# DeltaNet projections of one hybrid layer as seven half-size block products per slab, with sums and joining on VectorE

## The reference, cut to what matters

```python
proj = x @ w_in                        # x 256x2048, w_in 2048 x 18496
qkv = silu(causal_depthwise_conv(qkv, conv_w))           # 4 taps
q = l2_normalize(qkv[..., :2048] per head of 128)
k = l2_normalize(qkv[..., 2048:4096] per head of 128)
v = qkv[..., 4096:]                    # 32 heads of 128
...
o = chunked_gated_delta_rule(q, k, v, g, beta)
o = o * rsqrt(mean(square(o), axis=-1) + 1e-6)
o = o * norm_w * silu(z)               # z: another 4096 columns of proj
return o.reshape(...) @ w_dn_out
...
y = gelu(s5 output); (y @ w_glu_a) * sigmoid(y @ w_glu_b)    # the GLU stage
```

## Time and profile before

| | |
|---|---|
| median of 3 executions | 2885.38 us (2883.77 to 2957.61) |
| the profiled execution's own time | 2883.57 us |
| its span in the trace | 2881.8 us |
| mean granted TensorE clock | 0.995 of full speed (2.4 GHz) |
| TensorE busy | 2823.4 us, 98% of the span |
| weight loads busy | 2060.2 us, 71% |
| VectorE busy | 1038.6 us, 36% |
| ScalarE busy | 488.3 us, 17% |
| GpSimd busy | 75.2 us, 3% |

### The profile page before, as it was taken

The page is one execution under the profiler, slowest core; times in us unless marked ns, Lnnn a source line. Parts: engine busy times, 40 slices in busy tenths (PEclk is TensorE's granted clock), DMA queues, the critical chain, the costliest instruction groups (busy, mean ns, idle before and its releaser), DMA issues.

```text
span 2881.8 us, 50108 instructions
## 1 busy us (share of the span) xinstructions
PE 2823.4 (98%) x20775; PEld 2060.2 (71%) x20775; DVE 1038.6 (36%) x2273; ACT 488.3 (17%) x805; POOL 75.2 (3%) x119
## 2 busy tenths in 40 slices
PE   8999999999999999999989999999999999999997
PEld 7888888888888888888889999863444444434442
DVE  2433424424334306777765653221111121112114
ACT  2221232212312121110010000121111211112110
POOL 1000000000000000000010000000000000000000
PEclk9999999999999999999999999999999999999999
DMA  7243342332424534344447657277999999999997
GB/s 206 83 132 93 104 127 89 118 118 89 147 89 105 161 93 142 118 139 128 145 156 230 204 172 265 102 310 325 392 422 422 422 422 422 422 422 422 422 422 281
DMA packets 328853, 654.13 MB, mean 227 GB/s; under 512 B 45232, under 2 KB 274736, under 8 KB 279536
## 3 DMA queue, kind: packets, MB, share of 16 engines
q1 hardware_dynamic: 328688, 651.61, 61.6%
HBM read 649.49 MB, written 2.10 MB: 226 GB/s over the span
## 4 chain that ended last, share of the span: by engine, by line
PE 71%; issue 16%; DMA 7%; DVE 2%; DVEq 1%; POOLq 1%; SPq 1%; ACT 1%; ACTq 0%; POOL 0%
PE bank L670 14%; PE bank L999 10%; PE bank L1191 9%; PE bank L920 8%; PE bank L1229 7%; DMA arena<-in_w_up_dram 7%; PE bank L1170 4%; PE bank L1056 4%; PE bank L1269 4%; PE bank L746 1%; PE bank L764 1%; PE bank L757 1%; PE bank L883 1%; PE bank L1201 1%; POOLq L605 1%
## 5 line engine op out<-in xcount | busy, mean ns | idle before, releaser
L670 PE MATMUL bank<-arena 128*128 128x256 f32 x4096 | 931.1, 382 | 0.0
L670 PEld LDWEIGHTS bank<-arena 128*128 128x128 f32 x4096 | 763.7, 190 | 111.1 <-issue 7.6
L1191 PE MATMUL bank<-arena 128*64 128x512 f32 x2048 | 445.6, 594 | 12.5 <-DMA arena<-in_w_up_dram 12.5
L1191 PEld LDWEIGHTS bank<-arena 128*64 128x64 f32 x2048 | 144.3, 137 | 311.7 <-issue 281.6
L999 PE MATMUL bank<-arena 128*128 128x128 f32 x2576 | 290.1, 276 | 6.0 <-DVEq L1969 6.0
L999 PEld LDWEIGHTS bank<-arena 128*128 128x128 f32 x2576 | 289.9, 193 | 6.3 <-DVEq L1969 6.2
L920 PE MATMUL bank<-arena 128*128 128x256 f32 x1024 | 223.5, 380 | 0.0
L920 PEld LDWEIGHTS bank<-arena 128*128 128x128 f32 x1024 | 194.1, 190 | 26.6
L1229 PE MATMUL bank<-arena 128*64 128x512 f32 x960 | 209.3, 594 | 0.5 <-ACT arena L1580 0.5
L2229 DVE TENSOR_SCALAR arena<-bank 128x512 f32<-128x512 f32 x16 | 11.1, 691 | 463.2 <-PE bank L1191 463.2
L1229 PEld LDWEIGHTS bank<-arena 128*64 128x64 f32 x960 | 67.5, 137 | 131.7 <-issue 131.0
(11 more groups left out here) (336 smaller groups left out, 2076.7 us busy)
## 6 DMA issues: line engine op xcount, KB each, us to landing
arena<-in_w_in_dram SPq DMA_DIRECT2D x72, 2048.0 KB, 8.7
arena<-in_w_up_dram SPq DMA_DIRECT2D x64, 2048.0 KB, 16.5
arena<-in_w_gate_dram SPq DMA_DIRECT2D x64, 2048.0 KB, 13.9
arena<-in_w_down_dram SPq DMA_DIRECT2D x64, 2048.0 KB, 21.1
arena<-in_w_dn_out_dram SPq DMA_DIRECT2D x16, 2048.0 KB, 8.1
arena<-in_w_glu_b_dram SPq DMA_DIRECT2D x8, 2048.0 KB, 8.1
arena<-in_w_glu_a_dram SPq DMA_DIRECT2D x8, 2048.0 KB, 8.2
arena<-in_w_mix_out_dram SPq DMA_DIRECT2D x8, 2048.0 KB, 13.7
```

Source lines behind the costliest of these rows:

```text
L670: last = mm(ps[bank][:, ct * T:ct * T + T], ring[:, buf, k, ct * P:ct * P + P], rhs[:, k, :], start=k == 0, stop=k == KD - 1)
L1191: last = mm(ps[bank][CAP * o:CAP * o + CAP, :], xg[:, 4 * q + k, CAP * o:CAP * o + CAP], w[:, o, k], start=False, stop=q == 3 and k == 3, ...
```

## The change

Slabs 0 to 3 of each group are computed by seven block products each (`seven_heads`, 56 matmuls of 128 columns), with the parts in regions of banks 0, 1, 5, 6 and 1, 2, 0, 7. Their weight sums are built on VectorE (`sums`; for slab 0 of the next group in three pieces within the apply part, for slab 1 before the last scaling, for slabs 2 and 3 between the convolutions), the token sums of x once at the start (`token_sums`), and `join_heads` adds the parts up into `dn_joined` in SBUF, from which `conv` now reads. z slabs stay as they were.

The outputs of the apply part are now made with tokens on the partitions (operands swapped). So the sum of squares is a reduction on VectorE over ScalarE's squares (no product with ones), its rsqrt works on 8 elements per partition, VectorE scales into `otok`, and TensorE turns the eight blocks (`turn_outputs`) behind slab 0 of the next group. In the GLU stage the token sums of x move from GpSimd to VectorE, behind the weight sums of the second slab. The first load of the S5 slabs is issued ahead of the small S5 loads. VectorE's loop over the groups is written as seven turns and a last one.

```diff
+            def turn_outputs(g):
+                pe.wait_ge(apply_dve, 4 * g + 4)
+                for a in range(GV):
+                    for c in range(2):
+                        col = (a % 2) * T + c * P
+                        last = tr(ps[3 + a // 2][:, col:col + P], otok[:, c, a], ident[:, :])
+                last.then_inc(apply_pe, 1)
+
+            def seven_heads(g, r, lo, hi):
+                buf = r % RING
+                extra_w = dn_wsum[r % 2]
+                if lo == 0:
+                    pe.wait_ge(slot_loaded[buf], 16 * (2 * g + r // 3 + 1))
+                    pe.wait_ge(bank_taken[r % 3], 2 * g + r // 3 + 1)
...
+                table = ((0, weight(0, 0), plain(0, 0)), (1, weight(0, 1), plain(1, 0)),
+                         (6, summed(extra_w, 0), summed(dn_xsum, 0)), (2, summed(extra_w, 1), summed(dn_xsum, 1)),
+                         (5, weight(1, 0), summed(dn_xsum, 2)), (3, weight(1, 1), summed(dn_xsum, 3)),
+                         (4, summed(extra_w, 2), plain(1, 1)))
+                for i in range(lo, hi):
+                    if i == KD:
+                        pe.wait_ge(prepared, 4 * g + 2 + r)
+                    p, k = divmod(i, KD // 2)
...
             def front(g):
-                part(16 * (2 * g + 1), 0, 0, 2 * g, xT, 4, 2 * KD)
-                for r in range(1, 3):
-                    project(16 * (2 * g + 1), r, r, 2 * g, xT)
+                seven_heads(g, 0, 8, 56)
+                turn_outputs(g - 1)
+                seven_heads(g, 1, 0, 56)
+                seven_heads(g, 2, 0, 56)
...
-                part(16 * (2 * g + 2), 0, 0, 2 * g + 1, xT, 0, 18)
+                seven_heads(g, 3, 0, 36)
...
-                part(16 * (2 * g + 2), 0, 0, 2 * g + 1, xT, 18, 2 * KD)
+                seven_heads(g, 3, 36, 56)
                 pe.wait_ge(tok_taken, g + 1)
                 decay_products(1)
+                pe.wait_ge(bank_taken[2], 2 * g + 2)
                 z0(0, 19)
...
-                pe.wait_ge(osq_ready, g + 1)
-                for i in range(2):
-                    last = mm(ps[3 + i][:, :], ones[:, :], sq[:, i * 512:i * 512 + 512], start=True, stop=True)
-                last.then_inc(oss_ready, 1)
...
+            dve.wait_ge(xt_taken, 8)
+            token_sums(xT, dn_xsum)
+            sums(0, 0)
             dve.wait_ge(bd_ready, 1)
             dve.wait_ge(bias_loaded, 32)
...
             dve.sem_inc(glog_ready, 1)
+            sums(0, 1)
             dve.wait_ge(gcum_ready, 1)
...
+                join_heads(0)
                 conv(0)
+                sums(g, 2)
+                join_heads(1)
                 conv(1)
+                sums(g, 3)
+                join_heads(2)
                 conv(2)
...
                 decay(0)
+                join_heads(3)
                 conv(3)
                 decay(1)
...
+                if more:
+                    sums_one(g + 1, 0)
...
+                if more:
+                    sums_two(g + 1, 0)
...
+                if more:
+                    sums_three(g + 1, 0)
+
+                dve.wait_ge(osq_ready, g + 1)
+                V.tensor_reduce(osum, sq.rearrange("p (a t) -> p a t", t=P), AX_X, ALU.add)
+                dve.drain()
+                dve.sem_inc(oss_ready, 1)
                 dve.wait_ge(orn_ready, g + 1)
-                og = oT[:, ds(GV * g, GV), :]
-                V.tensor_tensor(og, og, rn.rearrange("p (a t) -> p a t", a=GV), ALU.mult)
-                dve.drain()
+                for c in range(2):
+                    V.tensor_tensor(otok[:, c], ps[7 - c][:, :].rearrange("p (a d) -> p a d", a=GV),
+                                    by_head(osum[:, GV * c:GV * c + GV], P), ALU.mult)
+                dve.drain()
+                dve.sem_inc(apply_dve, 1)
+                if more:
+                    sums(g + 1, 1)
                 dve.wait_ge(bank_taken[2], 2 * g + 3)
+                dve.wait_ge(apply_pe, 7 * g + 7)
...
-            weight_sums(1, 0, 1, True)
-            gelu_sums()
-            weight_sums(2, 0, 2, True)
+            weight_sums(0, 1, True)
+            dve.wait_ge(gelu_done, 1)
+            token_sums(uT, usum)
+            weight_sums(0, 2, True)
+            token_sums(xT, xsum)
             join(0, 1, True)
```

More of the change, by code:

```diff
@@ L161, in build @@
         zvT = at(w0 + 8192, GV, T)
+        dn_joined = at(w0, 512)
+        dn_partial = at(w0 + 512, 4, P)
+        dn_xsum = at(12288, 4, KD // 2, P)
+        dn_wsum = [at(w0 + 9216 + 3072 * i, 3, KD // 2, P) for i in range(2)]
+        regions = banks[:, :].rearrange("p (b n) -> p b n", n=P)
+        dn_first, dn_second = (0, 5, 1, 0), (1, 6, 2, 7)
         uT = at(SH, KD, T)
@@ L376, in _ @@
             sp.dma_start(dsk, d_skip.rearrange("(k a) q -> (a q) k", k=KD), allow_slow_non_contiguous=True).then_inc(s5_loaded, 16)
-            for r in range(3):
+            for r in range(1, 3):
                 load_slot((S_U + r) % RING, in_rows(w_in[:, SC * r:SC * r + SC]), r, U_USE)
@@ new lines, in seven_heads, with weight, plain, summed @@
+            def seven_heads(g, r, lo, hi):
[4 more added lines that the diff above has]
+                    pe.wait_ge(bank_taken[r % 3], 2 * g + r // 3 + 1)
+                    if r == 0:
+                        pe.wait_ge(bank_taken[1], 2 * g + 1)
+                    if r == 2:
+                        pe.wait_ge(bank_taken[0], 2 * g + 2)
+                        pe.wait_ge(bank_taken[1], 2 * g + 1)
+                    if r == 3:
+                        pe.wait_ge(kd_in, 1)
+                def weight(i, j):
+                    return lambda k: ring[:, buf, 8 * j + k, P * i:P * i + P]
+                def plain(i, j):
+                    return lambda k: xT[:, 8 * i + k, P * j:P * j + P]
+                def summed(v, i):
+                    return lambda k: v[:, i, k]
+                table = ((0, weight(0, 0), plain(0, 0)), (1, weight(0, 1), plain(1, 0)),
[6 more added lines that the diff above has]
+                    p, k = divmod(i, KD // 2)
+                    place, left, right = table[p]
+                    bank = dn_first[r] if place < 4 else dn_second[r]
+                    last = mm(regions[:, 4 * bank + place % 4], left(k), right(k), start=k == 0, stop=k == KD // 2 - 1)
+                if hi == 56:
+                    last.then_inc(bank_ready[r % 3], 1)
@@ L681, in group @@
+            def front(g):
+                seven_heads(g, 0, 8, 56)
+                turn_outputs(g - 1)
+                seven_heads(g, 1, 0, 56)
+                seven_heads(g, 2, 0, 56)
+            def group(g, more):
                 pe.wait_ge(sq_ready, g + 1)
@@ L1394, in _ @@
                 act.wait_ge(oss_ready, g + 1)
-                for i in range(2):
-                    A(rn[:, i * 512:i * 512 + 512], ps[3 + i][:, :], ACT.Ln, scale=1.0 / P, bias=eps_l2)
+                A(osum, osum, ACT.Ln, scale=1.0 / P, bias=eps_l2)
                 act.drain()
-                A(rn, rn, ACT.Exp, scale=-0.5).then_inc(orn_ready, 1)
+                A(osum, osum, ACT.Exp, scale=-0.5)
+                act.drain()
+                act.sem_inc(orn_ready, 1)
             act.sem_inc(phase_done[0], 1)
```

164 lines of the change are left out of this document (99 added, 65 removed).

## The result

The changed kernel takes 2870.05 us, the median of five executions (2868.29 to 2872.03), against 2885.38 us before: a ratio of 0.9949, 95% interval 0.9935 to 0.9962 (one slow execution of before, 2957.61 us, is left out of the ratio). It is faster by 15 us, where 36 were forecast, and 4 us outside the range.

The account below looks back on a forecast made before the run. TensorE's stream, busy 98% of the span, was taken as the bound. Savings of 41.6 + 6.0 + 6.0 less losses of 14.4 and 2.8 give 36.4 us, so 2849 us against 2885.38; 8-in-10 range 2833 to 2866 us.

Parts of the forecast that it names:

- The slab at 12.51 us: Slabs 0 to 3 of each group: 12.51 us each in seven products instead of 13.81, saving 41.6 us over 32 slabs.
- The outputs by token: Apply part's outputs: products with ones go (1.72 us per group), eight transposes come (0.97 us); 6.0 us saved.
- Weight sums at 1.23 us: Sign to look for: VectorE's weight sums run undisturbed at 1.23 us; sums over 2 us would show the prediction wrong.
- VectorE up by 214 us: Sign to look for: VectorE's busy time rises by some 27 us a group, about 220 us.
- `front`'s margins of 0.6 to 3.2 us: VectorE's sums, joins and scalings in `front` finish before TensorE wants them, with 0.6, 1.8 and 3.2 us to spare, costing nothing.
- the prologue: Start of the kernel: waits for decay biases (1.3 us) and for sums of slabs 1 and 2 (0.9, 0.6); 2.8 us lost.
- The joins in `front`: Sign to look for: VectorE's joins in `front` stand 12.5 us apart.
- The wait at the first level: Solve's first level: join(3) lengthens VectorE's chain, so TensorE's wait grows by 1.8 us per group; 14.4 us lost.
- rival (b): VectorE also late in `front` or at the scaling of q and k, 2 us per group more: 2865 us; chance 0.12.
- (c): New VectorE sums run at the disturbed 3.33 us beside GpSimd, not 1.23: 115 us more, 2964 us; chance 0.03.
- the term for the GLU stage: GLU stage: TensorE's 6.02 us wait for the token sums of y goes whole; 6.0 us saved.
- TensorE's rows follow each other without gaps: Within a group TensorE's stream is unbroken, the one wait being 0.20 us at the solve's first level.

Follow-up runs that it names:

- the delayed old kernel: Kernel before the change, with decay(1) computed three times over, which delays VectorE's chain to the solve's first level: 2907.48 us (1.008 of before).
- the filler in place: Changed kernel with TensorE's loop written out and four wide matmuls of z1 moved ahead of the transposes of v: 2829.71 us (0.9812 of before).

## Why the prediction was wrong

**What held.** The slab at 12.51 us and the 41.6 us from it. The outputs by token: 0.87 us of turns for 1.72 of products gives 6.8 us where I had 6.0. Weight sums at 1.23 us, VectorE up by 214 us, and `front`'s margins of 0.6 to 3.2 us: the sums' semaphore holds TensorE up only twice, 1.0 us in all, at 42 and 55 us, which are two terms of the prologue. (The joins in `front` stand 11.4 us apart and not 12.5 as I had written: behind a late first one VectorE works them off at its own pace.) The prologue: L734 comes at 64.43 us, 1.02 us earlier than L683 did, where 3.9 saved less 2.8 lost makes 1.1. The wait at the first level: 2.0 us in each group, 13.5 us more in all, where the sum had 14.4. Of rival (b), VectorE late in other places, no more was seen than that 1.0 us, though its 2865 us are nearest to the result; of (c), disturbed sums, nothing either.

**The sum left out what a wait costs behind it.** The step reads "the wait grows by 1.8 us per group: 14.4 us lost". The wait was right, but seven times TensorE then ran at the 1.2 GHz level for 3.4 us, six of them behind this wait: 6 x 1.5 and 1.75 for the one behind the jump, 10.8 us. (The written-out loop, with the same waits and only two spells, shows that the wait alone doesn't decide; without the loop's breaks this term would have been some 3 us.) The same omission made the term for the GLU stage too small, 6.0 where the wait and its 2.0 us at half speed make 8.0 and the stage gained 8.3. The row of before that would have told me is the granted clock behind the earlier trace rows; I read that row's wait and didn't look at the clock after it.

**The sum had no term for the jump.** "TensorE's rows follow each other without gaps" was true of before, and I carried it over. But slab 2 is what stands ahead of the loop's jump. With 64 wide records there the jump is hidden, with 224 narrow ones it isn't, and it costs 2.5 us, six times: 15.3 us. I costed the narrow records by their pitch alone and not by what they had been covering.

The account between the spans: 36.4 us predicted, less 15.3 for the jump and 10.8 for the clock, and 0.8, 2.3 and 0.9 better at the turns, the GLU stage and the wait: 14.3 us, against 13.5 measured. With the jump taken out the kernel is at 2848.17 us, which is the forecast's number in part by luck: what the GLU stage, the turns and the wait gave beyond their terms and two spells of low clock nearly cancel.

**What stays open.** Why the jump in the group loop costs 2.5 us and the GLU stage's loop, whose records are just as narrow, has no break in 2576 records; the two differ in that the GLU loop's body is short. Why 38 wide records ahead of the jump were not enough when 64 are. Why some waits of 2 us lower the clock and others of 2 us in the same place don't, and why more of them do when the loop has its breaks.

## What to carry to other kernels

When work in a saturated stream gets shorter, ask what its length was covering: here 64 wide records ahead of a loop's jump, and a chain on VectorE with 0.2 us to spare. Price a new wait on TensorE with its tail: in the delayed old kernel 14.6 us of waiting brought 8.5 us of low clock, so where a chain has become 2 us too long, put an equal piece of filler ahead of it, taken from where no load hangs on it. And where a loop turns only a few times, try it written out before looking for anything subtle: that one line was worth 22 us, more than the whole change, and with the filler in place 40.

## What was unexpected of the hardware

- A loop's jump on TensorE stopped the stream for 1.4 to 2.4 us (2.5 a jump on average with what follows) behind 128-column records and for 1.2 to 1.6 us behind 38 records of 256 columns, and not at all behind 64 of them.
- Waits of 2 us were enough for 3.4 us at half the clock, but only behind five of eight such waits in one kernel, six of eight in another and two of eight in a third.
- With weights arriving at 350 GB/s TensorE stood still for up to 2.5 us at a time among records of 64 columns, behind instruction packets that started up to 3.4 us later than without the load; with the load left at its old place in the stream it did not.
- The four-tap convolution took 0.62 us for its first pair of instructions from SBUF where it had taken 0.88 from a bank, and 2.27 us instead of 0.88 for the next pair when GpSimd was reading SBUF at the same time.
